# Two more gate tiles as a quad of block products in a one-core decoder layer

## The chip, the cores and the metric

The kernel runs on one core of a Trainium2 chip. The metric is the time of one execution on the device, in microseconds (us), from the kernel's first to its last work. The kernel before was run three times; its median is 1761.79 us.

## What is computed

One layer of a decoder on 1024 tokens of width 1024, all float32. Cut to what matters here:

```python
xn = rms_norm(x, g_pre_mix)
z  = xn @ w_in          # columns: q | k | v | conv B, C, h | pool u | 3 branch gates of 1024
y_attn = diff_attention(q, k, v, lam, subln_g)               # 8 heads, causal
gates  = sigmoid(z[..., OFF_GATE:] + b_gate)                  # (tokens, 3, 1024)
merged = gates[0] * (y_attn @ w_attn_proj) + gates[1] * (y_conv @ w_conv_proj) \
       + gates[2] * (y_pool @ w_pool_proj)
x = x + rms_norm(merged @ w_out, g_post_mix)
x = x + rms_norm(swiglu(rms_norm(x, g_pre_ffn)), g_post_ffn)
```

## The kernel before

**Precision and tiles.** Each operand is kept as a rounded high part (HH) and the rest, the low part (LL); a product is three passes of TensorE (PE), high by high, high by low, low by high. ScalarE (ACT) writes high parts (`copy`, L943), VectorE (DVE) subtracts to get low ones (`lo`, L1540). `xn`, normalized and transposed, stays in SBUF as [128, part, 8 blocks of k, 1024 tokens]. A tile of 128 output columns is a job: for each half of the tokens one group of 8 x 3 = 24 matmuls with 512 columns into one PSUM bank, 48 in all (`job`, `half_job`, `group`, L2306).

**Quads.** Most columns of z behind the attention are made in pairs of tiles instead, 256 columns by 1024 tokens: 2 x 2 blocks of weights against 2 x 2 blocks of `xn`, by 7 products in place of 8 (`x_quad` on each engine, the products at L2509, 12 matmuls each). This needs four sums S1 to S4 of blocks of `xn`, made once (`s_raw`, split into `s_op`, 2048 columns each), and for every quad four sums T1 to T4 of weight blocks (`x_sum`, L1761, 128x512), seven blocks split into high and low (`x_op`), and the weights themselves (`x_pair`, 1 MB, loaded by SyncE). PE works a quad in this order: T3 by S3, B11, then the last product (B22) of the quad before, B21, T2 by S2, T4, T1 by S1. ACT copies partial results out of PSUM (`x_b1`, `x_a1`, `x_a2`), and PE may not start the T2 product before `x_a1` is copied, since it goes on in the same bank. DVE combines, ACT makes the sigmoids, GpSimd (POOL) stores the parts to `gate_scratch`. The table `XQ` (L362) lists the quads. Of the first branch's gates, tiles 0 to 5 are made directly and the quad of tiles 6 and 7 comes first in `XQ`.

**Order of the work.** All engines have a hand-written order. For each head there are 8 steps (`step_of`): row block i of the scores, row minima and `e_t` on DVE, transposes by PE, and weighted values, with the next head's projections as fill for PE. Gates 0 and 1 are the fill of the last head (`gates_raw`). Behind it comes the drain, four steps with `lag` 1 to 4 that end the last head's rows (`y_row`, `y_out`), with gate tiles 2 and 3 as PE's fill. Then PE made tiles 4 and 5 (two `job(xn)`), and beside these DVE and ACT made the S and T sums and the operands of the first quad. Then come the 16 quads.

**Memory and its waits.** `y_out` (two heads in turn) lies at RM, the sigmoids' `stage` and the raw T sums (`x_raw`) lie on the same bytes. `merged` holds the gates 0 to 3 until they are stored to `gate_scratch`; the quads' `x_b1`, `x_a1`, `x_a2` lie where gate 0 and 1 did, so that ACT waits before its first quad for the four stores, and POOL's `pads_ready` does too:

```python
act.wait_ge(early_stored[0], 16 * 4)
for q in range(NQ):
    x_quad(q)
```

POOL issued, behind the norms of the last head (`norm`, L713 to L715, its small steps on `o_scale`): the store of the last head's `y_out` (L722, once the last low part of `y_out` is written), the stores of gates 0 and 1 (L752), of 2 and 3 (L757), of 4 and 5 (L762, from `stage`). SyncE issued the first two `x_pair` (L516) once the last `y_out` was written.

Of the kernel before, what the change touches and what calls it, by code (L numbers as in the profile page):

```python
# [73 lines left out]
def build(nc, x, g_pre_mix, w_in, b_gate, lambda_q1, lambda_k1, lambda_q2, lambda_k2, subln_g,  # L74
# [21 lines left out]
    G_TAIL = 2 * TT + 8  # L96
# [7 lines left out]
    with ctx:  # L104
# [19 lines left out]
        def const(name, shape, dt=F32):  # L124
# [45 lines left out]
                 for j, name in enumerate(("T1", "T2", "T3", "T4"))}  # L170

# [135 lines left out]
        early_stored = [sem(f"early_stored{i}") for i in range(2)]  # L307
# [54 lines left out]
        XQ = [("G", OFF_GATE + 6 * P, 6 * P)]  # L362
# [6 lines left out]
        X_QUAD_BANKS = (BANKS[1], BANKS[0])  # L369
# [98 lines left out]
        def _(sp):  # L468
# [155 lines left out]
        def _(pool):  # L624
# [123 lines left out]
            store_y(1, HEADS - 1)  # L748

            pool.wait_ge(gates_first, 2)  # L750
            for m in range(2):
                pool.dma_start(gate_dram[P * m:P * (m + 1), :], merged[:, m, :]).then_inc(early_stored[0], 16)  # L752
            for m in (2, 3):
# [3 lines left out]
                pool.dma_start(gate_dram[P * m:P * (m + 1), :], merged[:, m, :]).then_inc(early_stored[0], 16)  # L757
# [179 lines left out]
        def _(act):  # L937
# [215 lines left out]
            step_of(0, 0, lag=1)  # L1153
            gates_half(2, 0)
            step_of(0, 1, lag=2)
            gates_half(2, 1)
            split_next()
            step_of(0, 2, lag=3)
            gates_half(3, 0)
            step_of(0, 3, lag=4)  # L1160

            gates_half(3, 1)
            pr, sums_n = Count(), Count()

            def x_hi_of(name, q, summed=False):

                if summed:
                    act.wait_ge(xt_summed, sums_n.at(1))  # L1170
                    sums_n.next()
                    src = x_raw[name][:, :, :]
# [16 lines left out]
            def direct_part(q):  # L1189
# [5 lines left out]
                if q == 0:  # L1195
                    act.wait_ge(early_stored[1], 32)
                else:
                    wait_for(act, stage_stored[2], 16 * quads_of("GU", q))
                    wait_for(act, direct_dve, quads_of("HB", q))
# [46 lines left out]
            act.wait_ge(gates_first, 2)  # L1246
            act.wait_ge(xs_summed, 2)
            x_s_hi(3)
            split_next()
            act.wait_ge(xs_summed, 3)  # L1250
            x_s_hi(1)
            x_s_hi(2)
            act.wait_ge(y_stored[0], 16 * HEADS // 2)
            sigmoid_half(part_of(stage, 0, 0), bias_g[:, 4:5])
            act.wait_ge(x_pair_landed[0], 16)
            x_hi_of("T3", 0, True)
            x_hi_of("B11", 0)
            sigmoid_half(part_of(stage, 0, 1), bias_g[:, 4:5])
            act.wait_ge(xs_summed, 4)
            x_s_hi(4)  # L1260
            act.wait_ge(groups_done, g.at())
            x_hi_of("B21", 0)
            x_hi_of("T2", 0, True)
            for half in range(2):
                sigmoid_half(part_of(stage, 1, half), bias_g[:, 5:6])
            x_hi_of("T4", 0, True)
            act.wait_ge(early_stored[0], 16 * 4)
# [259 lines left out]
        def _(dve):  # L1527
# [144 lines left out]
            def step_of(par, i, lag=0, first=False, last=False):  # L1672
# [15 lines left out]
                if not lag:  # L1688
# [47 lines left out]
            step_of(0, 0, lag=1)  # L1736
            whole(s_raw[2][:, LL], xn, 0, 0)
            whole(s_raw[3][:, HH], xn, 0, 1)
            step_of(0, 1, lag=2)
            split_next()  # L1740
            x_s_sum(3, s_raw[2][:, LL], s_raw[3][:, HH], ALU.subtract)
            step_of(0, 2, lag=3)
            whole(s_raw[1][:, HH], xn, 1, 1)
            dve.wait_ge(pv_done, HEADS * TT)
            x_s_sum(1, s_raw[3][:, HH], s_raw[1][:, HH], ALU.add)
            step_of(0, 3, lag=4)
            g.next(4)
# [23 lines left out]
            def x_s_lo(kept, n_hi):  # L1771
                dve.wait_ge(xs_hi, n_hi)
                lo(s_op[kept][:, LL], s_raw[kept][:, LL], s_op[kept][:, HH]).then_inc(xs_lo, 1)

            def x_combine(q, turn, c, half, bank, kept, n_copy):
# [5 lines left out]
                elif q == 0:  # L1781
                    dve.wait_ge(early_stored[1], 32)
# [34 lines left out]
            def x_quad(q):  # L1817
# [3 lines left out]
                x_lo_of("T1", q)  # L1821
                if not last:
# [29 lines left out]
            dve.wait_ge(xs_summed, 2)  # L1852
            x_s_sum(2, s_raw[1][:, LL], s_raw[2][:, LL], ALU.subtract)
            x_s_lo(3, 1)
            split_next()
            dve.wait_ge(x_pair_landed[0], 16)
            dve.wait_ge(y_stored[1], 16 * HEADS // 2)
            x_sum("T3", 0)
            x_sum("T2", 0)
            x_sum("T4", 0)  # L1860
            x_sum("T1", 0)
            dve.wait_ge(xs_summed, 3)
            x_s_lo(1, 2)
            whole(s_raw[4][:, HH], xn, 1, 0)
            x_s_sum(4, s_raw[4][:, HH], s_raw[2][:, LL], ALU.subtract)
            x_lo_of("T3", 0)
            x_lo_of("B11", 0)
            dve.wait_ge(xs_summed, 4)
            x_s_lo(2, 3)
            x_lo_of("B21", 0)  # L1870
            x_lo_of("T2", 0)
            x_lo_of("T4", 0)
            x_s_lo(4, 4)
            g.next(4)
# [410 lines left out]
        def _(pe):  # L2285
# [216 lines left out]
            def x_sums(j):  # L2502
                return lambda s, k: s_op[j][:, s, k, :]
# [271 lines left out]
```

## Time and profile before

| what | value |
|---|---|
| median of three runs | 1761.79 us (1761.66 to 1762.31) |
| the profiled execution, its own time | 1761.83 us |
| its span | 1760.2 us |
| mean granted clock of TensorE | 0.999 |
| PE busy | 1749.9 us of the span |
| DVE busy | 1138.2 us |
| ACT busy | 737.2 us |
| POOL busy | 248.0 us |

The span runs from the first to the last instruction in the profile; the time of the execution is 1.6 us longer. A busy time is the sum over an engine's instructions. Times in the rows below are in us from the start of the span, so that rows of different engines can be laid side by side. An entry in square brackets at the end of a row is the time that the engine sat idle before it and what released it.

### The profile page before, as it was taken

The page shows a single profiled execution, that of the slowest core. Times are in us where ns is not written, and L with a number is a line of the kernel's source. Part 1 is how long each engine was busy: PE and PEld are TensorE (multiplying, and loading weights), DVE is VectorE, ACT ScalarE, POOL GpSimd, SP SyncE. Part 2 cuts the span into 40 slices and gives each one's busy share as a digit, 9 for nine tenths or more (in the row PEclk, how much of TensorE's full clock was granted, in tenths as well). Part 3 has the DMA queues.
Part 4 walks back from the last instruction along what each step waited for, and adds up shares of the span by engine and source line. Part 5 has one row for each costly group of instructions (what it writes and reads, how often), then busy time and mean ns, then how long its engine had stood idle before and what let it go on. Part 6 is the DMA issues. An engine that isn't in the chain of part 4 may idle for free.

```text
span 1760.2 us, 23940 instructions
## 1 busy us (share of the span) xinstructions
PE 1749.9 (99%) x8485; PEld 1452.2 (82%) x8485; DVE 1138.2 (65%) x1942; ACT 737.2 (42%) x1494; POOL 248.0 (14%) x554
## 2 busy tenths in 40 slices
PE   9999999999999999999999999999999999999998
PEld 7888888888888888888888888888888888888886
DVE  5328888888785764543465645886656655567676
ACT  5316666666643233343231123443333333344553
POOL 3321222222210001111100112100011000000011
PEclk9999999999999999999999999999999999999999
DMA  7421222222133223337635712233233223673443
GB/s 243 144 85 52 75 74 76 74 73 72 49 144 96 72 66 117 117 102 245 233 122 166 246 56 92 72 114 120 95 107 113 101 89 104 230 276 99 145 143 127
DMA packets 136671, 212.49 MB, mean 121 GB/s; under 512 B 7537, under 2 KB 93041, under 8 KB 135554
## 3 DMA queue, kind: packets, MB, share of 16 engines
q1 hardware_dynamic: 108160, 108.54, 19.7%
q0 software_dynamic: 28416, 102.73, 16.2%
q8 instruction: 55, 0.90, 0.2%
q14 instruction: 38, 0.31, 0.1%
q10 hardware_dynamic: 2, 0.00, 0.0%
HBM read 149.12 MB, written 62.13 MB: 120 GB/s over the span
## 4 chain that ended last, share of the span: by engine, by line
PE 98%; DVE 1%; ACT 1%; DMA 0%; issue 0%; POOL 0%; POOLq 0%; DVEq 0%; ACTq 0%
PE ps L2306 25%; PE ps L2638 22%; PE ps L2509 17%; PE ps L2718 12%; PE ps L2390 10%; PE ps L2314 3%; PE ps L2406 3%; PE ps L2428 2%; PE ps L2430 1%; PE ps L2649 0%; DMA x_tile<-in_x_dram 0%; DVE ring L1540 0%; ACT e_t L1064 0%; ACT ring L943 0%; PE ps L2653 0%
## 5 line engine op out<-in xcount | busy, mean ns | idle before, releaser
L2718 PE MATMUL ps<-d_op 128*128 128x512 f32 x924 | 210.3, 389 | 0.1
L2718 PEld LDWEIGHTS ps<-d_op 128*128 128x128 f32 x924 | 173.3, 188 | 36.8 <-DVE d_op L1540 0.5
L2638 PE MATMUL ps<-s_op,t_op_T 128*128 128x512 f32 x720 | 169.9, 389 | 0.0
L2390 PE MATMUL ps<-xn,ring 128*128 128x512 f32 x672 | 167.0, 398 | 0.0
L2638 PEld LDWEIGHTS ps<-s_op,t_op_T 128*128 128x128 f32 x720 | 135.1, 188 | 28.1
L2390 PEld LDWEIGHTS ps<-xn,ring 128*128 128x128 f32 x672 | 122.3, 188 | 24.2
L2509 PE MATMUL ps<-s_op,x_op_T 128*128 128x512 f32 x576 | 135.9, 389 | 0.0
L2509 PEld LDWEIGHTS ps<-s_op,x_op_T 128*128 128x128 f32 x576 | 108.2, 188 | 22.4
L2638 PE MATMUL ps<-hn,t_op_B 128*128 128x512 f32 x504 | 120.9, 389 | 0.0
L2638 PEld LDWEIGHTS ps<-hn,t_op_B 128*128 128x128 f32 x504 | 94.6, 188 | 19.6
L1652 DVE CUSTOM_DVE_ANT_0 ps<-ps,mask 128x256 f32<-128x256 f32 (+7 forms) x128 | 94.3, 778 | 12.2 <-PE ps L2406 11.2
L1540 DVE TENSOR_TENSOR t_op_B<-pair,t_op_B 128x512 fp32r<-128x512 f32 x63 | 43.3, 689 | 90.5 <-ACT t_op_B L943 90.5
L943 ACT ACTIVATE d_op<-rf_pieces 128x512 fp32r<-128x512 f32 x87 | 53.8, 630 | 106.6 <-PE ps L2718 101.0
L1540 DVE TENSOR_TENSOR d_op<-rf_pieces,d_op 128x512 fp32r<-128x512 f32 x87 | 59.2, 691 | 59.9 <-ACT d_op L943 59.9
L1064 ACT ACTIVATE e_t<-ps,neg_max 128x256 f32<-128x256 f32 (+7 forms) x128 | 93.9, 744 | 2.9 <-DVE neg_max L1652 2.9
L2509 PE MATMUL ps<-xn,x_op_B 128*128 128x512 f32 x384 | 92.1, 389 | 0.0
L2306 PE MATMUL ps<-w_v,xn 128*128 128x512 f32 x384 | 90.7, 396 | 0.0
L2306 PE MATMUL ps<-w_o,ring 128*128 128x512 f32 x384 | 89.0, 391 | 0.0
L2306 PE MATMUL ps<-ya,ring 128*128 128x512 f32 x384 | 87.9, 389 | 0.0
L2306 PEld LDWEIGHTS ps<-w_v,xn 128*128 128x128 f32 x384 | 72.6, 191 | 15.2 <-DVE xn L1540 0.3
L2509 PEld LDWEIGHTS ps<-xn,x_op_B 128*128 128x128 f32 x384 | 72.1, 188 | 14.9
L2306 PEld LDWEIGHTS ps<-ya,ring 128*128 128x128 f32 x384 | 72.1, 188 | 14.9
(269 smaller groups left out, 3355.0 us busy)
## 6 DMA issues: line engine op xcount, KB each, us to landing
pair<-in_w_gate_up_dram SPq DMA_DIRECT2D x21, 1024.0 KB, 5.2
rf_pieces<-s_scratch SPq DMA_DIRECT2D x77, 256.0 KB, 2.7
x_pair<-in_w_in_dram SPq DMA_DIRECT2D x16, 1024.0 KB, 6.6
raw<-in_w_in_dram SPq DMA_DIRECT2D x26, 512.0 KB, 4.1
s_scratch<-gated_ff POOLq DMA_DIRECT2D x44, 256.0 KB, 2.5
gate_in<-gate_scratch POOLq DMA_DIRECT2D x18, 512.0 KB, 3.6
s_scratch<-hf_out POOLq DMA_DIRECT2D x33, 256.0 KB, 2.4
v_scratch<-v_out POOLq DMA_DIRECT2D x32, 256.0 KB, 2.6
```

Of the source, the lines that this page charges most:

```text
L943: return act.activation(dst, src, ACT.Copy, **kw)
L1064: act.activation(e_t[:, i % 2, c, 0:w], score_row(i, c), ACT.Exp, bias=neg_max[:, i % 2, c:c + 1], scale=-1.0, accum_out=sums[:, i % 4, c: ...
L1540: return dve.tensor_tensor(dst, src, hi.bitcast(F32), ALU.subtract)
L1652: dve.tensor_tensor_reduce(out=scores, in0=scores, in1=mask[:, S - w:S], scale=-1.0, scalar=HIGHEST, op0=ALU.add, op1=ALU.min, accum_out=n ...
L2306: last = pe.matmul(ps[:, bank, :], lhs, rhs, start=i == 0, stop=i == len(pairs) - 1)
L2314: last = pe.transpose(ps[:, TB[b], P * k:P * (k + 1)], src[:, P * k:P * (k + 1)], ident[:, :])
L2390: last = pe.matmul(ps[:, proj_bank(first, half), :], proj_weights(which, par, a)[:, P * k:P * (k + 1)], xn[:, b, k, HALF * half:HALF * (ha ...
L2406: last = pe.matmul(score_row(i, c)[:, HALF * chunk:HALF * chunk + w], qt[rows, par, a, P * i:P * (i + 1)], kt[rows, par, b, HALF * chunk:H ...
L2428: pe.matmul(ps[:, U_BANK, 0:2 * HV], pt[:, i % 2, HH, k, :], vh[:, par, :, k, :], start=k == 0, stop=k == i, skip_group_check=True)
L2509: last = pe.matmul(ps[:, bank, :], x_op[name][:, a, k, :], block(b, k), start=opens and (k, a, b) == (0, HH, HH), stop=(k, a, b) == (3, LL ...
L2638: last = pe.matmul(ps[:, bank, :], t_op[name][:, a, k, :], block(b, k), start=opens and (k, a, b) == (0, HH, HH), stop=(k, a, b) == (3, LL ...
L2718: last = pe.matmul(ps[:, DOWN_BANKS[product][i], :], d_op[:, g % 4, a, P * i:P * (i + 1)], d_op[:, g % 4, 2 + b, :], start=opens and (a, b ...
```

## The change

Gate tiles 4 and 5 become a quad of their own, the first in `XQ`, so there are 17. Everything that quad needs before its first product is made earlier:

- The two whole blocks of `xn` in S3 are summed in quarters of 128x512 in the last head's steps on DVE (`quarter`), eight of them.
- S3, S1, S2 and the T sums of quad 0 are made in the drain's steps on DVE, S4 behind the drain; ACT's high parts likewise. The T sums of quad 0 have their own place (`x_raw_0`), the other half of `y_out`.
- SyncE issues `x_pair` 0 after the last row minimum (`max_ready`), `x_pair` 1 still after the last `y_out`.
- POOL stores gates 0 and 1 ahead of the last head's `y_out`. The stores of tiles 4 and 5 go with the quad's parts. `early_stored` is one semaphore for the four stores of gates 0 to 3.
- The direct jobs of tiles 4 and 5, their ring loads and splits, and their sigmoids are gone.

```diff
-        XQ = [("G", OFF_GATE + 6 * P, 6 * P)]
+        XQ = [("G", OFF_GATE + 4 * P, 4 * P), ("G", OFF_GATE + 6 * P, 6 * P)]
...
-        X_QUAD_BANKS = (BANKS[1], BANKS[0])
+        X_QUAD_BANKS = (BANKS[0], BANKS[1])
...
-            for j in range(6):
+            for j in range(4):
                 load(tile_of(w_in, OFF_GATE + P * j))
 
             for q, (kind, col, _) in enumerate(XQ):
-                if q < 2:
+                if q == 0:
                     for b in range(2):
                         sp.wait_ge(v_landed[b], 32 * HEADS // 2)
+                    sp.wait_ge(max_ready, 2 * HEADS * TT)
+                elif q == 1:
                     sp.wait_ge(tr_free[0], TT + HEADS * TT)
                     sp.wait_ge(tr_free[1], TT + HEADS * (TT + TT // 2))
...
-            store_y(1, HEADS - 1)
-
             pool.wait_ge(gates_first, 2)
             for m in range(2):
-                pool.dma_start(gate_dram[P * m:P * (m + 1), :], merged[:, m, :]).then_inc(early_stored[0], 16)
+                pool.dma_start(gate_dram[P * m:P * (m + 1), :], merged[:, m, :]).then_inc(early_stored, 16)
+            store_y(1, HEADS - 1)
...
-            for m in (4, 5):
-                for half in range(2):
-                    gi = 2 * TT + 2 * (m - 2) + half
-                    pool.wait_ge(evacuated[gi % 4], gi // 4 + 1)
-                pool.dma_start(gate_dram[P * m:P * (m + 1), :], stage[:, m - 4, :]).then_inc(early_stored[1], 16)
-            pool.wait_ge(early_stored[0], 16 * 4)
+            pool.wait_ge(early_stored, 16 * 4)
...
             step_of(0, 0, lag=1)
             gates_half(2, 0)
             step_of(0, 1, lag=2)
             gates_half(2, 1)
-            split_next()
+            act.wait_ge(gates_first, 2)
+            act.wait_ge(xs_summed, 3)
+            x_s_hi(3)
+            act.wait_ge(x_pair_landed[0], 16)
+            x_hi_of("T3", 0, True)
+            x_hi_of("B11", 0)
             step_of(0, 2, lag=3)
             gates_half(3, 0)
             step_of(0, 3, lag=4)
+            x_s_hi(2)
+            x_hi_of("B21", 0)
+            x_hi_of("T2", 0, True)
             gates_half(3, 1)
+            act.wait_ge(pv_done, HEADS * TT)
+            x_s_hi(1)
+            x_hi_of("T4", 0, True)
+            act.wait_ge(xs_summed, 4)
+            x_s_hi(4)
...
+            def quarter(dst, half, k):
+
+                s = slice(HALF * half, HALF * (half + 1))
+                dve.tensor_tensor(dst[:, k, :], xn[:, HH, k, s].bitcast(F32), xn[:, LL, k, s].bitcast(F32), ALU.add)\
+                    .then_inc(dve_step, 1)
+                step.next()
...
+                if last and i < 3:
+                    quarter(s_raw[3][:, HH], 0, i)
...
+                if ahead:
+                    ahead()
...
+                if last and i == 1:
+                    quarter(s_raw[3][:, HH], 0, 3)
+                if last and 2 <= i < 6:
+                    if i == 2:
+                        dve.wait_ge(pv_done, (HEADS - 1) * TT)
+                    quarter(s_raw[1][:, HH], 1, i - 2)
...
+            step_of(0, 0, lag=1, ahead=second_whole)
+            x_s_sum(3, s_raw[3][:, HH], s_raw[1][:, HH], ALU.subtract)
+            dve.wait_ge(xs_summed, 1)
+            dve.tensor_tensor(s_raw[1][:, HH], s_raw[1][:, HH], s_raw[2][:, LL], ALU.add).then_inc(xs_summed, 1)
+            step_of(0, 1, lag=2, ahead=sum_s2)
+            dve.wait_ge(x_pair_landed[0], 16)
+            dve.wait_ge(y_stored[0], 16 * HEADS // 2)
+            x_sum("T3", 0)
+            x_sum("T2", 0)
+            x_sum("T4", 0)
+            x_sum("T1", 0)
+            step_of(0, 2, lag=3)
+            x_s_lo(3, 1)
+            x_lo_of("T3", 0)
+            x_lo_of("B11", 0)
+            step_of(0, 3, lag=4)
+            g.next(4)
+            dve.wait_ge(pv_done, HEADS * TT)
+            whole(s_raw[4][:, HH], xn, 1, 0)
+            dve.wait_ge(xs_summed, 3)
+            x_s_sum(4, s_raw[4][:, HH], s_raw[2][:, LL], ALU.subtract)
+            x_lo_of("B21", 0)
+            x_lo_of("T2", 0)
+            dve.wait_ge(xs_summed, 4)
+            x_s_lo(2, 2)
+            x_lo_of("T4", 0)
+            x_s_lo(1, 3)
...
                 x_lo_of("T1", q)
+                if q == 0:
+                    x_s_lo(4, 4)
+                    dve.wait_ge(y_stored[1], 16 * HEADS // 2)
...
-            for _ in range(2):
-                job(xn)
             for b in range(2):
                 pe.wait_ge(tr_free[b], tr[b].at())
+            pe.wait_ge(u_ready, HEADS * TT)
```

How PE's order reads from the last rows of the drain to the first quad. Before:

```order
L2314 MATMUL ps<-ident_148,y_row_109 128x128
L2306 MATMUL ps<-xn_49,ring_133 128x512 x114
L2509 MATMUL ps<-s_op3_51,x_op_T3_82 128x512 x12
L2509 MATMUL ps<-xn_49,x_op_B11_83 128x512 x12
L2509 MATMUL ps<-xn_49,x_op_B21_84 128x512 x12
```

With the change:

```order
L2325 MATMUL ps<-ident_152,y_row_113 128x128
L2317 MATMUL ps<-xn_49,ring_137 128x512 x18
L2520 MATMUL ps<-s_op3_51,x_op_T3_82 128x512 x12
L2520 MATMUL ps<-xn_49,x_op_B11_83 128x512 x12
L2520 MATMUL ps<-xn_49,x_op_B21_84 128x512 x12
L2520 MATMUL ps<-s_op2_52,x_op_T2_85 128x512 x12
```

Only 18 matmuls of tile 3 are left between the last transpose and the T3 product; the 96 of tiles 4 and 5 are gone from here.

How ACT's order reads ahead of the first copies of the first quad, with the semaphores that a row waits for (`s_op` is the high part of an S sum, `x_b1` and `x_a1` the copies out of PSUM). Before:

```order
L1046 ACTIVATE stage_95<-ps,bias_g_150 128x512 [waits groups_done]
L943 ACTIVATE s_op4_54<-s_raw4_58 128x2048 [waits xs_summed]
L943 ACTIVATE x_op_B21_84<-x_pair0_89 128x512 [waits groups_done]
L943 ACTIVATE x_op_T2_85<-x_raw_T2_97 128x512 [waits xt_summed]
L1046 ACTIVATE stage_95<-ps,bias_g_150 128x512 [waits groups_done] x2
L943 ACTIVATE x_op_T4_86<-x_raw_T4_99 128x512 [waits xt_summed]
L943 ACTIVATE x_b1_91<-ps 128x512 [waits x_products,early_stored0]
```

With the change:

```order
L945 ACTIVATE s_op2_52<-s_raw2_56 128x2048
L945 ACTIVATE x_op_B21_84<-x_pair0_89 128x512
L945 ACTIVATE x_op_T2_85<-x_raw_0_T2_101 128x512 [waits xt_summed]
L1048 ACTIVATE merged_117<-ps,bias_g_154 128x512 [waits groups_done]
L945 ACTIVATE s_op1_53<-s_raw1_57 128x2048 [waits pv_done]
L945 ACTIVATE x_op_T4_86<-x_raw_0_T4_103 128x512 [waits xt_summed]
L945 ACTIVATE s_op4_54<-s_raw4_58 128x2048 [waits xs_summed]
L945 ACTIVATE x_b1_91<-ps 128x512 [waits x_products,early_stored]
L945 ACTIVATE x_op_T1_87<-x_raw_0_T1_100 128x512 [waits xt_summed]
L945 ACTIVATE x_a1_92<-ps 128x512 [waits x_products]
```

Behind the sigmoid of gate 3 (the row that writes `merged`) four rows are left before `x_b1` and its wait for the stores; before, the sigmoids of tiles 4 and 5 (the rows that write `stage`) and all of the S high parts stood between them.

## Rows read from the trace of the kernel before

**Rows 1.** The page, parts 1 and 4: busy time; the chain that ended last.
```profile
PE 1749.9 (99%) x8485; PEld 1452.2 (82%) x8485; DVE 1138.2 (65%) x1942; ACT 737.2 (42%) x1494; POOL 248.0 (14%) x554
...
PE 98%; DVE 1%; ACT 1%; DMA 0%; issue 0%; POOL 0%; POOLq 0%; DVEq 0%; ACTq 0%
```

**Rows 2.** Timeline of PE, tile 3 to the first product: start, us, engine, what.
```profile
494.63 26.13 PE L2306 MATMUL ps<-xn,ring 128*128 128x512 f32 x114
520.60 2.88 PE L2509 MATMUL ps<-s_op,x_op_T 128*128 128x512 f32 x12
523.32 5.60 PE L2509 MATMUL ps<-xn,x_op_B 128*128 128x512 f32 x24
```

**Rows 3.** Timelines of PE and DVE in the last head, steps i = 2 and 3.
```profile
444.60 0.49 PE L2314 MATMUL ps<-ident,e_t 128*128 128x128 f32 x3
...
443.33 0.17 DVE L1638 RECIPROCAL rsums<-sums 128x2 f32<-128x2 f32 x1 [0.48 <-ACT e_t L1064]
...
443.84 0.62 DVE L1643 SCALAR_TENSOR_TENSOR e_t<-e_t,d_scale 128x384 f32<-128x384 f32 x1
```

**Rows 4.** Timeline of DVE behind the last head.
```profile
481.01 4.61 DVE L1729 TENSOR_TENSOR s_raw<-xn 128x2048 f32<-128x2048 f32 x2
...
498.71 0.28 DVE L1540 TENSOR_TENSOR y_out<-ps,y_out 128x128 fp32r<-128x128 f32 x1
...
503.77 1.22 DVE L1540 TENSOR_TENSOR ring<-raw,ring 128x1024 fp32r<-128x1024 f32 x1
```

**Rows 5.** The same timeline: the first x_sum, a sum of 128x512.
```profile
509.03 0.69 DVE L1761 TENSOR_TENSOR x_raw_T<-x_pair 128x512 f32<-128x512 f32 x1 [4.04 <-DMA y_scratch<-y_out]
```

**Rows 6.** Timeline of POOL behind the last head.
```profile
483.43 2.60 POOL L714 TENSOR_TENSOR o_scale<-o_scale,minus_half 128x1 f32<-128x1 f32 x1
...
489.18 0.55 POOL L714 TENSOR_TENSOR o_scale<-o_scale,minus_half 128x1 f32<-128x1 f32 x1
...
499.29 0.63 POOL L722 DMA_DIRECT2D y_scratch<-y_out  x1 [9.29 <-DVE y_out L1540]
499.92 1.06 POOL L752 DMA_DIRECT2D gate_scratch<-merged  x2
500.97 1.05 POOL L757 DMA_DIRECT2D gate_scratch<-merged  x2
512.56 0.54 POOL L762 DMA_DIRECT2D gate_scratch<-stage  x1 [10.54 <-issue]
```

**Rows 7.** Timeline of ACT behind the last head.
```profile
499.04 0.69 ACT L1046 ACTIVATE merged<-ps,bias_g 128x512 f32<-128x512 f32 x1 [3.85 <-PE ps L2306]
...
523.58 0.60 ACT L943 ACTIVATE x_b<-ps 128x512 f32<-128x512 f32 x1 [0.41 <-PE ps L2509]
...
526.24 0.60 ACT L943 ACTIVATE x_a<-ps 128x512 f32<-128x512 f32 x1 [1.54 <-PE ps L2509]
```

**Rows 8.** Tiles merged (gates 0 to 3), then y_out: issue to landing.
```profile
DMA to landing us min/median/max: 10.6/12.3/14.0
...
DMA to landing us min/median/max: 4.2/4.2/9.6
```

**Rows 9.** DMA view of 499 to 504.3, then of 503 to 513.
```profile
q1 hardware_dynamic: 755, 0.77, 62.1%
...
x_pair<-in_w_in_dram SPq DMA_DIRECT2D x2, 1024.0 KB, 12.7
...
DMA packets 1741, 3.91 MB, mean 391 GB/s; under 512 B 78, under 2 KB 1193, under 8 KB 1613
...
gate_scratch<-stage POOLq DMA_DIRECT2D x1, 512.0 KB, 5.2
```

**Rows 10.** PE's last row; two late stretches, whose last columns are PEclk, DMA share, GB/s.
```profile
1737.74 15.49 PE L2718 MATMUL ps<-d_op 128*128 128x512 f32 x66
...
1757.40:1760.20 2.80, 0.00 (x0) 0.00 (x0) 0.35 (x1) 0.00 (x0) 0.00 (x0) 0.50 0.50 187
1752.00:1757.20 5.20, 1.23 (x6) 0.69 (x4) 4.44 (x7) 0.79 (x3) 2.58 (x4) 1.00 0.47 190
```

More of the change, by code:

```diff
@@ L170, in build @@
                  for j, name in enumerate(("T1", "T2", "T3", "T4"))}
+        x_raw_0 = {name: at(f"x_raw_0_{name}", [P, 4, P], F32, RM + 2048 * j)
+                   for j, name in enumerate(("T1", "T2", "T3", "T4"))}
         x_tile = at("x_tile", [P, 2, D], F32, RF)
@@ L306, in build @@
         sig_ready, conv_ready = sem("sig_ready"), sem("conv_ready")
-        early_stored = [sem(f"early_stored{i}") for i in range(2)]
+        early_stored = sem("early_stored")
         stage_stored = [sem(f"stage_stored{i}") for i in range(4)]
@@ L368, in build, with raw_sum @@
         NQ = len(XQ)
-        X_QUAD_BANKS = (BANKS[1], BANKS[0])
+        X_QUAD_BANKS = (BANKS[0], BANKS[1])
+        def raw_sum(name, q):
+            return (x_raw if q else x_raw_0)[name][:, :, :]
         def made(q, name):
@@ L1194, in direct_part @@
                     return
[L1195 to L1199, printed above, removed]
+                wait_for(act, stage_stored[2], 16 * quads_of("GU", q))
+                wait_for(act, direct_dve, quads_of("HB", q))
                 part, src = part_of(stage, 1, 0), ps[:, X_QUAD_BANKS[q % 2][0], :]
@@ L1244, in x_quad @@
                     sigmoid_part(q, 0, 1)
[L1246 to L1267, printed above, removed]
+            act.wait_ge(early_stored, 16 * 4)
             for q in range(NQ):
@@ L1670, in y_lo, with step_of @@
                 transposed_lo(1, lambda s: y_out[:, par, s, P * i:P * (i + 1)].rearrange("p (k t) -> p k t", t=P), 1)
-            def step_of(par, i, lag=0, first=False, last=False):
+            def quarter(dst, half, k):
[3 more added lines that the diff above has]
+                step.next()
+            def step_of(par, i, lag=0, first=False, last=False, ahead=None):
                 if not lag:
@@ L1757, in x_sum @@
                 in0, in1, op = {"T3": (corner(pair_x, "B22"), corner(pair_x, "B12"), ALU.subtract),
-                                "T2": (x_raw["T3"][:, :, :], corner(pair_x, "B11"), ALU.add),
-                                "T4": (corner(pair_x, "B21"), x_raw["T2"][:, :, :], ALU.subtract),
+                                "T2": (raw_sum("T3", q), corner(pair_x, "B11"), ALU.add),
+                                "T4": (corner(pair_x, "B21"), raw_sum("T2", q), ALU.subtract),
                                 "T1": (corner(pair_x, "B12"), corner(pair_x, "B11"), ALU.subtract)}[name]
-                dve.tensor_tensor(x_raw[name][:, :, :], in0, in1, op).then_inc(xt_summed, 1)
+                dve.tensor_tensor(raw_sum(name, q), in0, in1, op).then_inc(xt_summed, 1)
                 sums_n.next()
@@ L1766, in x_lo_of @@
                 dve.wait_ge(xt_hi, t_n.at(1))
-                src = x_raw[name][:, :, :] if name in x_raw else corner(x_pair[q % 2], name)
+                src = raw_sum(name, q) if name in x_raw else corner(x_pair[q % 2], name)
                 lo(x_op[name][:, LL], src, x_op[name][:, HH]).then_inc(xt_lo, 1)
@@ L1772, in x_s_lo, with second_whole, sum_s2 @@
                 dve.wait_ge(xs_hi, n_hi)
-                lo(s_op[kept][:, LL], s_raw[kept][:, LL], s_op[kept][:, HH]).then_inc(xs_lo, 1)
+                raw_at = HH if kept == 1 else LL
+                lo(s_op[kept][:, raw_at], s_raw[kept][:, raw_at], s_op[kept][:, 1 - raw_at]).then_inc(xs_lo, 1)
+            def second_whole():
+                dve.wait_ge(scores_done, HEADS * TT)
+                whole(s_raw[2][:, LL], xn, 1, 1)
+            def sum_s2():
+                dve.wait_ge(xs_summed, 2)
+                x_s_sum(2, s_raw[1][:, HH], s_raw[3][:, HH], ALU.subtract)
+            step_of(0, 0, lag=1, ahead=second_whole)
[9 more added lines that the diff above has]
+            x_sum("T1", 0)
+            step_of(0, 2, lag=3)
+            x_s_lo(3, 1)
+            x_lo_of("T3", 0)
+            x_lo_of("B11", 0)
+            step_of(0, 3, lag=4)
+            g.next(4)
[9 more added lines that the diff above has]
+            x_s_lo(1, 3)
             def x_combine(q, turn, c, half, bank, kept, n_copy):
@@ L1850, in x_quad @@
                 x_combine(q, 3, 1, 1, alpha, x_b1, 1)
[L1852 to L1874, printed above, removed]
             dve.wait_ge(small_landed, 16 * 5)
@@ L2502, in x_sums @@
             def x_sums(j):
-                return lambda s, k: s_op[j][:, s, k, :]
+                return lambda s, k: s_op[j][:, 1 - s if j == 1 else s, k, :]
             def x_product(bank, name, block, opens=False):
```

40 lines of the change are left out of this document (13 added, 27 removed).

## The prediction

> **What bounds the kernel now.** I read the page first. TensorE (PE) is busy 99% of the span of 1760.2 us, and the chain that ended last is 98% PE [rows 1]. So a change is worth the PE time that it takes away, less every wait that it puts in front of PE. Then the timeline of PE, for the place of the two gate tiles: one run of 114 matmuls starts at 494.63, and the first block product at 520.60, so a matmul takes 25.97 / 114 = 0.2278 us of PE. The 12 of that product take 523.32 - 520.60 = 2.72 us, 0.2267 each [rows 2]. Of the 114, 18 finish tile 3 and 96 are tiles 4 and 5. No row there names a releaser: PE waits for nothing. Last the timelines of the other engines beside this run, VectorE (DVE), ScalarE (ACT), GpSimd (POOL) and the DMA queues. They have until 520.6 to make the first quad's operands. The change takes that cover of 21.9 us away.
>
> The profiled execution took 1761.83 us against a median of 1761.79; I work from 1761.83, and the sum holds for both. A measurement of this kernel can tell about 0.2%, 3.5 us, from no change.
>
> **1. PE work.** Two tiles made directly are 2 x 48 = 96 matmuls, 96 x 0.2278 = 21.87 us. As a quad they are 7 products of 12, 84 x 0.2267 = 19.04 us. Everything else on PE stays. **-2.83 us**, and this is all that the change can gain.
>
> **2. The quarters in the last head.** DVE gets 8 sums of 128x512 there; such a sum of two SBUF tiles takes 0.69 us [rows 5], 5.5 us in all. PE waits for DVE where it transposes e_t. The difference of i = 2 ends at 443.84 + 0.62 = 444.46 and PE transposes at 444.60: 0.14 us to spare [rows 3]. Ahead of it stand two quarters close by (the end of step 1 and step 2), 1.38 us, with 0.48 us of idle just before it to swallow part [rows 3] and some more in front of y_row. I take 0.5 us of PE wait there. The six others stand in steps whose idle time covers them. **+0.5 us**; bounds 0 and 1.4 (two whole quarters uncovered).
>
> **3. The sums in the drain.** Before, DVE started its first two sums of 2048 columns at 481.01, 4.61 us for two [rows 4]. The new order from there, at these prices: S3 and the sum in place to 485.6; y_row at 486.4, since POOL's step on o_scale takes 2.60 us while such sums run, and 0.55 otherwise [rows 6]; S2 to 489.0; u_row and y_out 0.4; four x_sum of 0.69 [rows 5] to 492.1; y_row near 493; y_out of tile 6 after ACT at 494.0; the low half of S3 2.2, of T3 and B11 0.6 each, to 497.4; the last y_out to **497.7**, against 498.99 before [rows 4]. PE wants S3 and T3 at 494.63 + 18 x 0.2278 = 498.7: 1.9 us to spare. Then S4 in two sums to 502.2, B21 502.8 (wanted at 504.2), T2 503.4, S2 505.6 (wanted at 506.9), T4 506.2, S1 508.4 (wanted at 512.3). ACT's high halves run ahead of these, S4's to 504.1. So I cost the sums at nothing. Their cover is PE's three first products, thinnest at S2, 1.3 us; without it each sum would cost its 2.3.
>
> **4. The wait that loses its cover.** ACT's first copy of the quad phase, x_b1, waits for early_stored, the four stores of gates 0 to 3, because x_b1 and x_a1 lie where gate 0 does. PE may start the fourth product (T2) only after x_a1. Before, the four stores were issued at 499.92 to 501.5 and landed 10.6 to 14.0 us later, the last near 515.5 [rows 6, 8], and ACT made x_b1 at 523.58, when PE's product was ready: hidden by 8 us [rows 7]. Now T2 is due at 498.73 + 36 x 0.2267 = **506.9**, and gate 3 still isn't made before 499.04 + 0.69 = 499.73 [rows 7]. Gates 0 and 1 are now stored first, near 493, when no other transfer is out. At the last y_out, 497.7, SyncE issues x_pair 1 (1 MB) and POOL the stores of y (1 MB), of gate 2 and, near 500.3, of gate 3 (0.5 MB each), 3.15 MB (1 MB here is 1.05 of the profile's). After the like start of before, only the load's queue (q1) has a row in the first 5.3 us, 0.77 MB, and then all of them move 0.39 MB a us or a little more, 3.91 in 10 [rows 9]. Shifted by the 1.3 us that y_out is earlier: 0.77 MB by 503.0, and the other 2.38 MB take 5.9, to 508.9. With one load queued in place of two the first stretch may be some tenths shorter. I take **508.6**. Behind it ACT makes x_b1, T1's high half and x_a1, 0.5 to 0.6 each and 0.1 of waiting [rows 7]: 1.7 us. PE resumes at 510.3. **+3.4 us** of idle PE. Bounds: with the store of y as fast as its median (4.2 us [rows 8]) and the gates right behind it, the last lands near 505 and PE waits nothing; with 14.0 us for gate 3, as at worst before, it lands at 514.3, and PE waits 9. The value taken is nearer to the lower end, since 1 MB of x_pair 0 and 1 MB of gates 0 and 1 were in flight then and are not now.
> Queued behind ACT's wait are the high halves of T1, B22 and of the next quad's T3. DVE reaches T1 at 508.4 and waits for it, and there also for pads_ready, which POOL sets after the same stores. Both then run at least a product ahead of a PE that is 3.4 late, so they add nothing.
>
> **5. The rest.** SyncE issues x_pair 0 after the last row minimum (near 470) instead of the last y_out: it has 20 us and took 12.7 in the crowd [rows 9]. On that queue two ring loads are gone and nothing waits behind it but x_pair 1. The next quad's x_sum needs the store of y, which lands near 507.5; DVE comes to it at 512. Four sigmoids, two ring splits and two gate stores go, none on PE's path. The new quad's own combines, sigmoids and stores lie beside PE's products like those of the 16 others.
>
> **Sum:** -2.83 + 0.5 + 3.4 = +1.1, and 1761.83 + 1.1 = **1762.9 us**: no change that a measurement can tell.
>
> **A rule of the notes against the row.** The store of y, issued at 499.29, had moved nothing by 504.3 [rows 6, 9], and DVE was busy until 503.77 + 1.22 = 504.99 [rows 4]. A queue shared with a load and a store that is held up by DVE would both look so. The Trainium skill (SBUF — State Buffer, "SBUF: two separate sides") says that a DVE operation in a two-port mode keeps GpSimd from writing the descriptors of its own DMAs, while one with two SBUF inputs blocks only a GpSimd operation that reads SBUF. By its first half the stores would move only when DVE pauses (rival C); by its second half the slow o_scale step of point 3 is explained, and the stores are left alone.
>
> **Rivals.**
> A, the forecast: PE waits 2 to 5 us for the stores before T2.
> B, the stores land by 506. For it: y's median, and half the crowd gone. Against it: in the first 5 us only the load moved, at the same pair of issues. -2.83 + 0.5 + 0 to 0.9: 1759.5 to 1760.4.
> C, slower: from 497.7 DVE runs two-input sums without a pause until it lacks T1's high half, at 508.4, and that half waits for the stores. If POOL's stores can't begin while DVE is so busy, they begin there, need 2.1 MB / 0.4 = 5.3 us and 1 us to start, and ACT 1.7: PE resumes at 516.4, 9.5 us late, -2.83 + 0.5 + 9.5 = +7.2, **1769.0**. The verdict turns slower once PE waits over 5.9 us, which is when the stores have landed after 511.1. Against it: the store issued at 512.56 took 5.2 us to land while DVE was busy from 509.03 without a pause [rows 5, 6, 9].
> D, slower: PE idles, its clock falls, and it resumes at the lower of its two levels (1.2 GHz of 2.4). At the end of the span PE's last matmul ended at 1753.2, the granted clock was full until 1757.2, and half from 1757.4 on [rows 10]: 4 us of idleness lie before a fall. The forecast's wait is 3.4, so it decides only if the wait is longer than forecast. A product then takes 5.4 instead of 2.7 us; with one or two such, and a wait of 4.5, 1761.83 - 2.83 + 0.5 + 4.5 + 2.7 to 5.4 = 1766.7 to 1769.4. The Trainium skill (TensorE: Matmul & The Clock Gate, Part 1) has the clock fall after idleness too.
> E, the operands are late as well (POOL holds y_row up longer, the quarters cost more): 1 to 2 us more, 1764 to 1765.
>
> **Numbers.** A 0.58, B 0.21, E 0.11, C 0.06, D 0.04. The range runs from 1759.8 to 1765.3: C, D and about half of B are left out. Faster by over 3.5 us is out of reach, as the work taken away is 2.83: 0.01, for what I don't see. Slower by over 3.5: C, D and the tails of A and E, 0.11. Same: 0.88.
>
> **What would show it.** 84 instead of 96 matmuls between the same neighbours. PE idle for about 3.4 us, once, between the third and the fourth product, released by ACT's x_a; and ACT idle before x_b until a store of merged lands. Eight quarters of 0.69 us in the last head and some tenths of PE waiting for e_t. The last y_out near 498. I am wrong if T2 starts without a wait (B), if the wait is over 6 us (C), if PE waits before T3 (E), or if the granted clock dips behind the wait (D).

## The result and the profile after

| | before | after |
|---|---|---|
| median of 11 runs each, us | 1761.67 (1761.23 to 1762.32) | 1766.12 (1765.42 to 1766.69) |
| ratio after/before, 95% interval | | 1.0025 [1.0015, 1.0034] |
| profiled execution, its span | 1761.83, 1760.2 | 1765.44, 1763.9 |

The change costs 4.45 us, and the interval of the ratio lies above 1. The forecast was 1762.9 and the range ended at 1765.3; the time lies above both. The page of the kernel after, parts 1 and 4:

```profile
PE 1749.1 (99%) x8473; PEld 1450.6 (82%) x8473; DVE 1143.8 (65%) x1960; ACT 741.1 (42%) x1502; POOL 252.3 (14%) x556
...
PE 97%; DVE 1%; DMA 1%; ACT 1%; issue 0%; POOL 0%; POOLq 0%; DVEq 0%; ACTq 0%
```

PE has 12 matmuls fewer than in [rows 1], but its busy time fell by 0.8 us, not by 2.8, and DMA has come into the chain. PE's waits, with the total, the number and the longest:

```profile
PE ps L2520 <- ACT x_a L945: 4.4, 1, 4.4
PE ps L2358 <- POOL ident L652: 2.0, 1, 2.0
PE ps L2325 <- DVE e_t L1634: 0.9, 1, 0.9
```

The last two stood in the kernel before too, with the same lengths (a fourth, of 0.2 us at the start, is left out). One wait is new. PE's timeline from the last transpose on, to lay beside [rows 2]:

```profile
493.84 4.37 PE L2317 MATMUL ps<-xn,ring 128*128 128x512 f32 x18
498.05 2.88 PE L2520 MATMUL ps<-s_op,x_op_T 128*128 128x512 f32 x12
500.77 5.60 PE L2520 MATMUL ps<-xn,x_op_B 128*128 128x512 f32 x24
510.81 5.42 PE L2520 MATMUL ps<-s_op,x_op_T 128*128 128x512 f32 x12 [4.44 <-ACT x_a L945]
516.07 2.91 PE L2520 MATMUL ps<-xn,x_op_T 128*128 128x512 f32 x12
```

The first three products run as planned. T2 was due at 500.77 + 24 x 0.2267 = 506.21, the start that it would have had if PE had gone on without a pause. It starts at 510.81, **4.60 us late**. It then takes 516.07 - 510.81 = 5.26 us, where 12 matmuls take 2.72: **2.54 us more**. Stretches of this timeline; behind the length stand busy time of PE, PEld, DVE, ACT and POOL, then PEclk, DMA share, GB/s:

```profile
508.50:509.00 0.50, 0.00 (x0) 0.00 (x0) 0.00 (x0) 0.00 (x0) 0.00 (x0) 1.00 0.02 8
509.00:509.50 0.50, 0.00 (x0) 0.00 (x0) 0.00 (x0) 0.44 (x1) 0.10 (x1) 0.73 0.00 0
509.50:510.00 0.50, 0.00 (x0) 0.00 (x0) 0.00 (x0) 0.50 (x2) 0.00 (x0) 0.50 0.00 0
510.80:516.00 5.20, 5.19 (x12) 4.11 (x13) 5.11 (x7) 1.53 (x3) 0.00 (x0) 0.50 0.07 17
516.00:530.00 14.00, 14.00 (x63) 11.52 (x62) 6.68 (x11) 6.03 (x11) 1.64 (x3) 1.00 0.38 126
```

The granted clock falls to half, 1.2 GHz, about 3 us after PE went idle, and PE makes the whole T2 product at it. Why PE waited stands in the timelines of ACT and of POOL:

```profile
501.39 1.92 ACT L945 ACTIVATE s_op<-s_raw 128x2048 fp32r<-128x2048 f32 x1
509.06 0.60 ACT L945 ACTIVATE x_b<-ps 128x512 f32<-128x512 f32 x1 [5.75 <-DMA gate_scratch<-merged]
509.56 0.62 ACT L945 ACTIVATE x_op_T<-x_raw_T 128x512 fp32r<-128x512 f32 x1
510.08 0.59 ACT L945 ACTIVATE x_a<-ps 128x512 f32<-128x512 f32 x1
```

```profile
490.63 1.16 POOL L758 DMA_DIRECT2D gate_scratch<-merged  x2
497.13 0.53 POOL L730 DMA_DIRECT2D y_scratch<-y_out  x1 [5.33 <-DVE y_out L1531]
497.65 0.53 POOL L764 DMA_DIRECT2D gate_scratch<-merged  x1
499.47 0.53 POOL L764 DMA_DIRECT2D gate_scratch<-merged  x1 [1.29 <-ACT merged L1048]
509.09 0.10 POOL L766 MEMSET conv_in<- 128x4 f32 x1 [9.09 <-DMA gate_scratch<-merged]
```

ACT has the high part of S4 at 503.3 and then stands 5.75 us before `x_b1`, until the last of the four gate stores has landed; POOL's memset, behind the same stores, goes at the same moment. `x_b1`, T1's high part and `x_a1` take 1.6 us, and PE goes on at 510.8.

**The account.** -2.83 (96 matmuls against 84) + 4.60 (idle) + 2.54 (half clock) = +4.31, against 4.45 between the medians. In the two profiled executions the difference is 3.61: everything in the trace of after lies about 0.8 us earlier (its last transpose at 493.81, in the kernel before at 494.60), from the first 20 us of the kernel on, where both programs are alike. In the traces of this kernel and of those below that leave the quarters alone, with the same work on PE up to there, the T3 product starts anywhere from 498.05 to 498.96; no row gives a cause for this shift. So distances are taken within one trace, and where two traces are compared the shift is named.

### The profile page after: what moved, and what is told of

Read it like the earlier page. It is cut to its first block, busy times and chain, and to the rows that moved or that the text cites. A ratio compares the mean times of both kernels' runs of the same rounds, so it can differ in the third digit from the quotient of the medians.

```text
span 1763.9 us, 23944 instructions
## 1 busy us (share of the span) xinstructions
PE 1749.1 (99%) x8473; PEld 1450.6 (82%) x8473; DVE 1143.8 (65%) x1960; ACT 741.1 (42%) x1502; POOL 252.3 (14%) x556
## 4 chain that ended last, share of the span: by engine, by line
PE 97%; DVE 1%; DMA 1%; ACT 1%; issue 0%; POOL 0%; POOLq 0%; DVEq 0%; ACTq 0%
PE ps L2317 24%; PE ps L2649 22%; PE ps L2520 18%; PE ps L2729 12%; PE ps L2401 10%; PE ps L2325 3%; PE ps L2417 3%; PE ps L2439 2%; PE ps L2441 1%; DMA gate_scratch<-merged 1%; PE ps L2660 0%; DVE ring L1531 0%; DMA x_tile<-in_x_dram 0%; ACT e_t L1066 0%; ACT ring L945 0%
## 5 line engine op out<-in xcount | busy, mean ns | idle before, releaser
L2520 PE MATMUL ps<-s_op,x_op_T 128*128 128x512 f32 x612 | 147.0, 394 | 4.4 <-ACT x_a L945 4.4
L2520 PEld LDWEIGHTS ps<-s_op,x_op_T 128*128 128x128 f32 x612 | 116.4, 190 | 29.2 <-issue 4.8
L2520 PE MATMUL ps<-xn,x_op_B 128*128 128x512 f32 x408 | 97.8, 389 | 0.0
L2520 PEld LDWEIGHTS ps<-xn,x_op_B 128*128 128x128 f32 x408 | 76.6, 188 | 15.9
L1531 DVE TENSOR_TENSOR x_op_B<-x_pair,x_op_B 128x512 fp32r<-128x512 f32 x51 | 35.0, 690 | 79.9 <-ACT x_op_B L945 79.9
```

The lines of the kernel that those rows point to most:

```text
L1531: return dve.tensor_tensor(dst, src, hi.bitcast(F32), ALU.subtract)
L2520: last = pe.matmul(ps[:, bank, :], x_op[name][:, a, k, :], block(b, k), start=opens and (k, a, b) == (0, HH, HH), stop=(k, a, b) == (3, LL ...
```

## Experiments

Three questions: is it the wait of ACT for the stores, and for which of them; is it the clock; and what would be left of the gain without both. Each run is compared with runs of the kernel before on the same chip; their medians are 1761.67 and 1761.57.

### Waiting only for gates 0 and 1

`x_b1` and `x_a1` lie on gate 0 and `x_a2` on gate 1, so ACT needs only the first two stores. They get a semaphore of their own. DVE's wait for `pads_ready`, which POOL sets behind all four stores, moves to the third quad as well, so the run tells what both waits cost together:

```diff
-                pool.dma_start(gate_dram[P * m:P * (m + 1), :], merged[:, m, :]).then_inc(early_stored, 16)
+                pool.dma_start(gate_dram[P * m:P * (m + 1), :], merged[:, m, :]).then_inc(first_stored, 16)
...
-            act.wait_ge(early_stored, 16 * 4)
+            act.wait_ge(first_stored, 16 * 2)
...
-            dve.wait_ge(pads_ready, 1)
             for q in range(NQ):
+                if q == 2:
+                    dve.wait_ge(pads_ready, 1)
```

> The changed kernel, but ACT waits before the first quad only for the stores of gates 0 and 1 (a semaphore of their own), POOL's memset for all four, and DVE for that memset ahead of quad 2. If the wait for the stores of gates 2 and 3 (4.6 us) and the low clock behind it (2.5 us) are what the change lost, both go and the 2.83 us of matmuls stay: about 1759.0 us, no PE wait before the fourth product, granted clock full there. Rival, the sums of the last head and drain cost PE time too or come late: 1760 to 1763, with a PE wait before T3, S2 or T4. Rival, POOL's stores can't move while DVE sums: the store of y lands late and PE waits before the second quad's T3.

Measured: **1760.50** (1759.79 to 1760.86), 0.9993 [0.9984, 1.0002]. Against after that is 5.6 us less; every run of it (up to 1760.86) is below every run of before on the same chip (from 1761.03), though the interval still takes in 1. ACT makes `x_b1` at 504.14, T2 starts at 507.12 without a wait. But of the 2.83 us only 1.17 are there. PE and ACT, timelines:

```profile
509.84 2.88 PE L2522 MATMUL ps<-xn,x_op_T 128*128 128x512 f32 x12
513.71 5.69 PE L2522 MATMUL ps<-s_op,x_op_T 128*128 128x512 f32 x24 [0.99 <-ACT x_a L946]
```

```profile
511.93 0.63 ACT L946 ACTIVATE x_op_T<-x_raw_T 128x512 fp32r<-128x512 f32 x1 [5.69 <-DVE x_raw_T L1756]
512.47 0.61 ACT L946 ACTIVATE x_op_B<-x_pair 128x512 fp32r<-128x512 f32 x1
512.99 0.58 ACT L946 ACTIVATE x_a<-ps 128x512 f32<-128x512 f32 x1
```

T1 was due at 509.84 + 2.72 = 512.56 and comes 1.15 us late: the next wait. `x_a2` stands on ACT behind the high part of the next quad's T3, and that behind DVE, whose T3 sum (511.21) stands behind the low part of S4 (509.01, 2.28 us). In the kernel after, this was hidden in the 7 us that PE lost at T2. -2.83 + 1.15 would be 1.68 us of gain, 0.5 more than the medians have. In the traces that rest lies ahead of the first quad, in the shift named above, and has no cause shown.

### The same stores without the load beside them

ACT waits for all four stores as in the change; only the load of `x_pair` 1, which started with them, waits until they have landed:

```diff
                     sp.wait_ge(tr_free[1], TT + HEADS * (TT + TT // 2))
+                    sp.wait_ge(early_stored, 16 * 4)
```

> The changed kernel, but SyncE issues x_pair 1 only when the four gate stores have landed. If the stores are late because the load issued with them goes first (in the changed kernel the load's queue alone moved for 3.8 us), they begin 1.2 us after their issue, move 2.1 MB at 0.36 to 0.39 MB a us, land near 504.5, and PE waits nothing or a few tenths before T2; x_pair 1 lands near 511, before DVE wants it at 510 to 513: 1759 to 1761. Rival, DVE's two-input sums hold POOL's stores back: they begin as late as in the changed kernel (501.8 or later) and the time stays at 1765 to 1767.

Measured: **1760.59** (1759.77 to 1760.91), 0.9993 [0.9983, 1.0002], and T2 starts without a wait. POOL and ACT, timelines:

```profile
497.99 0.53 POOL L731 DMA_DIRECT2D y_scratch<-y_out  x1 [5.36 <-DVE y_out L1532]
...
500.32 0.53 POOL L765 DMA_DIRECT2D gate_scratch<-merged  x1 [1.28 <-ACT merged L1049]
504.81 0.10 POOL L767 MEMSET conv_in<- 128x4 f32 x1 [3.96 <-DMA gate_scratch<-merged]
```

```profile
504.79 0.60 ACT L946 ACTIVATE x_b<-ps 128x512 f32<-128x512 f32 x1 [0.61 <-DMA gate_scratch<-merged]
```

The last store lands 4.5 us after its issue at 500.32; with the load beside it, 9.6 us after (499.47 to 509.06). DVE does the same without a pause, sums with two SBUF inputs:

```profile
497.61 2.28 DVE L1738 TENSOR_TENSOR s_raw<-xn 128x2048 f32<-128x2048 f32 x1
499.93 2.29 DVE L1743 TENSOR_TENSOR s_raw<-s_raw,s_raw 128x2048 f32<-128x2048 f32 x1
```

So rival C falls: the stores move beside a busy DVE, and what held them up is the load. By the second half of the rule of the Trainium skill ("SBUF — State Buffer", "SBUF: two separate sides"), a DVE operation with two SBUF inputs blocks only a GpSimd operation that reads SBUF. This trace agrees: while DVE went on with such sums, the last gate store landed in 4.5 us. The 1.15 us before T1 are there again (T1 at 513.65, due at 512.50).

### The store of y ahead of gates 0 and 1

```diff
+            store_y(1, HEADS - 1)
             pool.wait_ge(gates_first, 2)
...
-            store_y(1, HEADS - 1)
```

> The changed kernel with one part undone: POOL stores y first and gates 0 and 1 behind it, so that 1 MB more stands in the queue ahead of gate 3. If the wait is set by what the queues have to move, the last gate lands 1.05 MB / 0.39 = 2.7 us later, PE waits 7.3 us before T2, and the clock falls as well: 1768.8. Rival, the wait is set by when the last gate is issued or by DVE: unchanged, 1766.

Measured: **1768.29** (1767.93 to 1768.98, 4 runs), 1.0039 [1.0024, 1.0054]. All 3 MB of stores and the load now start together:

```profile
512.42 0.60 ACT L945 ACTIVATE x_b<-ps 128x512 f32<-128x512 f32 x1 [8.42 <-DMA gate_scratch<-merged]
```

T2 was due at 506.88 and starts at 514.16, 7.28 late, and takes 4.37, 1.65 more than at full clock. -2.83 + 7.28 + 1.65 = +6.1, against 6.6. The more was queued ahead of the awaited store, the longer the wait. The early stores of gates 0 and 1, the part of the change that the prediction counted on, are worth some 2 us.

### The clock: matmuls in the wait

18 matmuls whose result nothing reads, ahead of the wait for `x_a1`; then 9 of them:

```diff
                 pe.wait_ge(xs_lo, 2)
+                if q == 0:
+                    wait_evacuated(pe, g, -2)
+                    for _ in range(18):
+                        pe.matmul(ps[:, 2, :], xn[:, HH, 0, 0:P], xn[:, HH, 0, 0:HALF], start=True, stop=True,
+                                  skip_group_check=True)
                 pe.wait_ge(x_copied, 3 * q + 2)
```

> The changed kernel, but before the wait ahead of the first T2 product PE makes 18 more matmuls of 512 columns into bank 2, whose result nothing reads (4.1 us of work in a wait of 4.6). If 2.5 us of the loss are matmuls at the lower clock behind an idle PE, the clock stays full, T2 still starts near 510.8 and takes 2.7 us in place of 5.3: 1763.5. If the long T2 product has another cause (say its S2 operand or a bank), it stays 5.3 long: 1766.

> The changed kernel with 9 idle-filling matmuls in place of 18 ahead of the first T2 product: PE is then idle 2.4 us instead of 4.4, with T2 starting at the same moment. If an idle stretch of 2.4 us does not lower the clock, the time is that of fill_18, 1763.9, with a T2 product of 2.7 to 3.0 us. If it does, as with no fill, 1765 to 1766.

Measured: 18 of them **1763.95** (1763.42 to 1764.52), 1.0013 [1.0004, 1.0022]; 9 of them **1763.55** (1763.18 to 1765.46), 1.0013 [1.0004, 1.0023]. PE in the first:

```profile
506.77 4.24 PE L2553 MATMUL ps<-xn 128*128 128x512 f32 x18
511.57 3.03 PE L2520 MATMUL ps<-s_op,x_op_T 128*128 128x512 f32 x12 [0.56 <-ACT x_a L945]
```

and in the second:

```profile
506.81 2.20 PE L2553 MATMUL ps<-xn 128*128 128x512 f32 x9
511.33 3.01 PE L2520 MATMUL ps<-s_op,x_op_T 128*128 128x512 f32 x12 [2.32 <-ACT x_a L945]
```

T2 starts 4.80 and 4.52 us late, as in after, but takes 2.87 and 2.85. Useless work in the wait makes the kernel 2.2 to 2.6 us faster: that is the price of the clock, and the 2.54 of the trace of after. With 9, PE stood idle for 2.3 us, and the granted clock of the traced run stayed at 1.00:

```profile
510.00:511.00 1.00, 0.00 (x0) 0.00 (x0) 0.08 (x1) 1.00 (x3) 0.00 (x0) 1.00 0.00 0
511.00:512.00 1.00, 0.67 (x3) 0.58 (x4) 1.00 (x2) 0.80 (x2) 0.00 (x0) 1.00 0.00 0
```

### The sum of the next quad ahead of S4's low part

On top of the first experiment, to take the second wait away:

```diff
                 if q == 0:
-                    x_s_lo(4, 4)
                     dve.wait_ge(y_stored[1], 16 * HEADS // 2)
                 if not last:
                     dve.wait_ge(x_pair_landed[(q + 1) % 2], 16 * ((q + 1) // 2 + 1))
                     x_sum("T3", q + 1)
+                if q == 0:
+                    x_s_lo(4, 4)
```

> The kernel two_sems with one move on DVE: in quad 0 the T3 sum of the next quad stands ahead of the low half of S4 instead of behind it. In two_sems PE still waited 1.1 us before the T1 product, for ACT's x_a2, which stood behind ACT's T3 copy of the next quad, which waited 5.7 us for that sum. If this row of waits is all that is left, T3's sum comes 2.2 us earlier, x_a2 is made right behind its product, the 1.1 us go and the full 2.83 us of matmuls show: 1761.7 - 2.8 = 1758.9 to 1759.3, no PE wait behind the drain. Rival, S4's low half or the next T3's low half comes too late instead: a PE wait before the second quad, 1760 or more.

Measured: **1758.75** (1758.35 to 1759.31), 0.9985 [0.9976, 0.9994]: faster than before by 2.8 us, the whole of the work taken away, and the fastest kernel here. PE goes through without a pause:

```profile
500.88 5.60 PE L2523 MATMUL ps<-xn,x_op_B 128*128 128x512 f32 x24
506.32 2.88 PE L2523 MATMUL ps<-s_op,x_op_T 128*128 128x512 f32 x12
509.04 2.88 PE L2523 MATMUL ps<-xn,x_op_T 128*128 128x512 f32 x12
511.76 5.60 PE L2523 MATMUL ps<-s_op,x_op_T 128*128 128x512 f32 x24
```

DVE's T3 sum is at 508.21 instead of 511.21, 0.8 us of it the shift between the two traces and 2.2 the move, and ACT has `x_a2` at 509.99 + 0.58 = 510.57, before T1 is due at 511.76. Each against its own before, this kernel gains 1.65 us on that of the first experiment: 1.15 are the wait, and the other 0.5 is the rest named there. Since the gain is the whole of the work taken away, neither the quarters nor the sums in the drain cost anything in this version.

### The quarters twice, and none

On top of the last kernel. First each quarter is made twice; then none, with the two sums made whole in the drain instead:

```diff
+                dve.tensor_tensor(dst[:, k, :], xn[:, HH, k, s].bitcast(F32), xn[:, LL, k, s].bitcast(F32), ALU.add)\
+                    .then_inc(dve_step, 1)
+                step.next()
+                dve.wait_ge(dve_step, step.at())
```

```diff
-                if last and i < 3:
-                    quarter(s_raw[3][:, HH], 0, i)
...
-                if last and i == 1:
-                    quarter(s_raw[3][:, HH], 0, 3)
-                if last and 2 <= i < 6:
-                    if i == 2:
-                        dve.wait_ge(pv_done, (HEADS - 1) * TT)
-                    quarter(s_raw[1][:, HH], 1, i - 2)
...
                 dve.wait_ge(scores_done, HEADS * TT)
+                whole(s_raw[3][:, HH], xn, 0, 0)
+                whole(s_raw[1][:, HH], xn, 0, 1)
                 whole(s_raw[2][:, LL], xn, 1, 1)
```

> The kernel sum_ahead with each of the eight quarters made twice in the last head (5.5 us more of DVE work, same result). The changed kernel showed no PE wait on the quarters where I had forecast 0.5 us, because ACT's e_t, not DVE, ended the wait for the difference. If a head's step has a further 0.7 us free on DVE, nothing changes: 1759. If not, PE waits some tenths at the steps i = 2 to 4, where two or three of them come close together: 1759.5 to 1761.

> The kernel sum_ahead with the quarters undone: DVE makes those two whole blocks of 2048 columns in the drain's first step instead (2 x 2.3 us). DVE's chain there had 1.9 us to spare before T3 and 1.3 before S2. 0.9 us of the 4.6 fall into DVE's idle time before u_row, so the rest comes some 3.7 us later: PE waits 1.8 us before T3 and about 0.6 more before S2: 1759 + 2.4 = 1761.4, as good as the kernel before. Rival, the drain has more slack than I read: 1759 to 1760.

Measured: twice **1762.64** (1762.09 to 1763.21), 1.0007 [0.9998, 1.0016], so 3.9 us above the kernel without the repeats, and more than was expected; none **1762.96** (1761.14 to 1763.91), 1.0006 [0.9997, 1.0016], 4.2 above. Neither interval excludes 1 against before, but every run of either lies above every run of the kernel that they start from (up to 1759.31). The last head with the quarters twice, PE, first step i = 2, then i = 6:

```profile
445.46 0.55 PE L2332 MATMUL ps<-ident,e_t 128*128 128x128 f32 x3 [1.18 <-DVE e_t L1635]
...
470.63 0.55 PE L2332 MATMUL ps<-ident,e_t 128*128 128x128 f32 x3 [0.66 <-DVE y_out L1532]
```

Eight more sums, 5.5 us of DVE, cost 3.7 us of PE by the T3 product (501.89 against 498.16, in traces that lie within 0.04 of each other at 430), half of it by step 3. From 440 to 450 DVE is busy 9.56 of 10 us and PE only 8.67, where with single quarters DVE has 9.15 and PE 10.00: DVE bounds that stretch. The first eight used up what slack there was.

Without quarters PE waits in the drain for the last `y_out`, and the clock falls; PE, then two stretches of the same trace:

```profile
497.03 0.45 PE L2322 MATMUL ps<-ident,y_row 128*128 128x128 f32 x1 [2.53 <-DVE y_out L1532]
497.12 5.85 PE L2314 MATMUL ps<-xn,ring 128*128 128x512 f32 x18
```

```profile
496.00:496.50 0.50, 0.00 (x0) 0.00 (x0) 0.00 (x0) 0.50 (x3) 0.00 (x0) 1.00 0.99 401
496.50:497.00 0.50, 0.00 (x0) 0.01 (x1) 0.41 (x2) 0.50 (x2) 0.00 (x0) 0.89 1.03 401
497.00:497.50 0.50, 0.47 (x2) 0.50 (x3) 0.50 (x1) 0.13 (x1) 0.00 (x0) 0.50 0.82 303
```

The transpose was due at 494.32, as 6 matmuls lie between the transposes and take 1.47 us, and starts 2.7 us late. The 18 matmuls take 502.81 - 497.12 = 5.69 us instead of 4.20. 2.7 of wait and 1.5 of clock are the 4.2 that were measured. The ten runs of this kernel fall into two groups, 3 at 1761.14 to 1761.57 and 7 at 1762.67 to 1763.91. The lower one is what the wait alone gives, 1758.75 + 2.7 = 1761.5. That the clock did not fall in those three is not shown, as the only trace is of a run of the upper group. It is argued from the sum and from the mean granted clock of the runs: 0.999 in all three of the lower group, 0.998 in five of the seven of the upper.

## Why the prediction was wrong, point by point

**What bounds the kernel, and point 1 (-2.83).** Right. PE is the bound, and with every wait of the change gone the kernel gains 2.8 us.

**Point 2 (+0.5 for the quarters).** Too dear: 0. In the trace of after PE waits for nothing in the last head that it did not wait for before. DVE's pauses took up the quarters: from 426 to 470 it waited 6.8 us for POOL, ACT and PE in the kernel before, and 3.1 us in after. The stretch in both, before first, with the busy time of PE, PEld and DVE:

```profile
426.00:470.00 44.00, 44.00 (x287) 37.16 (x286) 36.24 (x99) 28.94 (x85) 8.07 (x25) 1.00 0.13 46
426.00:470.00 44.00, 44.00 (x287) 37.15 (x286) 40.02 (x104) 28.96 (x83) 9.30 (x25) 1.00 0.10 37
```

That more would cost was seen rightly, and the twofold quarters show how close it was: 3.9 us for the second eight.

**Point 3 (the sums in the drain at nothing).** Right: PE waits for no operand. The last `y_out` was to end at 497.7; it ended at 496.83 in a trace that lies 0.8 earlier, 0.1 ahead of the plan, and S1's low half at 507.56 where the plan, so shifted, had 507.6. What the order of these sums cost shows only behind the first wait (below).

**Point 4 (+3.4 for the wait of `x_b1`).** Right in mechanism and place: one wait, before T2, released by `x_a`, set by the last gate store. It measured 4.60, 1.2 more. The queue behaved as in [rows 9], only more so. DMA view of after, from 497 to 502, then from 502 to 509:

```profile
q1 hardware_dynamic: 636, 0.65, 60.9%
q0 software_dynamic: 2, 0.02, 0.8%
...
q0 software_dynamic: 430, 2.08, 71.5%
q1 hardware_dynamic: 404, 0.40, 16.1%
```

By 502 the queues had moved 0.67 MB, where the shifted plan had 0.77 by 502.2, and the other 2.48 MB took 6.9 us, 0.36 MB a us instead of 0.40. The stores landed at 509.0 where the plan, shifted by 0.8, had 507.8. The remark that a shorter queue would make the first stretch shorter was wrong.

The sentence of the same point that what is queued behind "adds nothing" held for the kernel after only because the larger wait hid it. The prediction followed T1, B22 and pads_ready, but not `x_a2`, behind the next quad's T3 sum on DVE. It is worth 1.15 us as soon as the first wait is mended.

**The sum left the clock out.** This is the step that put the time outside the range: the term was put at nothing and measured 2.54. With 1.2 more at point 4 and 0.5 less at point 2 it makes the 3.2 us between forecast and result. Rival D had the mechanism and the price: a wait of 4.5 and one product at half clock give 1766.7, measured 1766.12; what it has too much is mostly the 0.5 for the quarters. But it stood at 0.04, because "4 us of idleness lie before a fall" was read from the end of the span [rows 10] as if it were a fixed length, and the forecast wait of 3.4 lay below it. In the trace of after about 3 us of idleness lay before the fall, in that of the kernel without quarters about 2.4, and in that with 9 fill matmuls 2.3 passed without one. One row was taken for a rule. Even at the forecast wait of 3.4 the fall could have come, and with it the sum would have been 1762.9 + 2.5 = 1765.4. The Trainium skill ("TensorE: Matmul & The Clock Gate", Part 1) has the clock fall after idleness. The trace agrees: the granted clock went from 1.00 to 0.50 behind the idle PE.

**Rivals.** A was right but for the clock; B needed the load away (shown: without it PE waits for nothing before T2, and the time is 1760.59, with 1.15 us of waiting for `x_a2` in it); C is refuted; D is what happened; E did not.

## What to carry to other kernels

Price a wait of TensorE twice: its length, and then the first product behind it at half clock. Here the clock had fallen behind waits of 2.5, 4.4 and 7.1 us, and not behind one of 2.3 in the traced run. When a stretch of work that covered the neighbours is taken away, list every wait on the other engines that ended inside it, each with its own due time, since the longest hides the others; and look at what a semaphore counts, as here waits for four stores, where two were needed, cost 5.6 us. A store that someone waits for should not be issued together with a load that nobody needs yet.

## What the runs showed that I had not expected

- Idle time before the granted clock fell was about 4.1 us at the end of the span, 3.6 with the store of y first, 3 in the kernel after, 2.4 without the quarters; 2.3 with 9 fill matmuls passed without a fall in the traced run, but two of the ten runs of that kernel are 1.5 and 1.9 us above its median. At this length it seems to fall in some runs and not in others.
- Back from idleness, PE ran at half clock for some 3 us in the kernel without quarters (497.0 to 500.3), for 3.3 with the store of y first (514.2 to 517.5) and for more than 5 in after (510.8 to 516), at steady work in all three.
- A load of 1 MB beside POOL's stores costs them more than its bytes. Without it 2.10 MB of stores were through between 498 and 505; with it they had moved 0.02 MB in the first 5 us, while the load itself moved at 0.13 MB a us and took 10.3 us where it took 5.5 alone. Which resource the two share stays open.
